# Query and key operands of the scores: transposed and split in the projection stage and stored, instead of in the attention stage

## What is computed

```python
xn = _rmsnorm(x, norm1_w)
proj = xn @ w_in
q, k, v, f_raw, z, xbc, dt_raw, g_att, g_ssm = _split_proj(proj)
q = _rmsnorm(q.reshape(b, T, 16, 64), q_norm_w)
k = _rmsnorm(k.reshape(b, T, 16, 64), k_norm_w)
logf = jax.nn.log_sigmoid(f_raw + b_f)
# attention, per head; c = cumsum(logf), for the running rows over the cached keys too
s = jnp.einsum('bqhd,bkhd->bhqk', q, k) * 64 ** -0.5
s = jnp.where(mask, s + (cq - ck), -jnp.inf)
att = softmax(s) @ v
```

## Time and profile before

| what | value |
|---|---|
| median of three runs | 2890.07 us (2890.05 to 2894.38) |
| the profiled execution's own time | 2885.89 us |
| its span, first to last instruction | 2884.1 us |
| PE busy over the span | 2737.1 us (95%) |
| DVE / ACT / POOL busy | 1577.2 (55%) / 1022.4 (35%) / 405.7 us (14%) |
| mean granted TensorE clock | 0.978 of full speed |
| DMA | 273.31 MB, mean 95 GB/s |

### The profile page before, as it was taken

One profiled execution on the slowest core, in us unless ns is written; L12 is line 12 of the kernel. 1 busy time (PEld: TensorE's weight loads), 2 busy tenths in 40 slices (PEclk: granted clock), 3 DMA queues, 4 the chain that ended last, 5 costly groups with the idle time before them and its releaser, 6 DMA issues. The chain is left out here.

```text
span 2884.1 us, 47789 instructions
## 1 busy us (share of the span) xinstructions
PE 2737.1 (95%) x18754; PEld 2658.0 (92%) x18754; DVE 1577.2 (55%) x2867; ACT 1022.4 (35%) x2353; POOL 405.7 (14%) x475
## 2 busy tenths in 40 slices
PE   6998979999999999997999989998989999999999
PEld 5997978989999889887999979998989999999999
DVE  4336337656566565565898864464373444434434
ACT  4223336556666655653434331121231111111110
POOL 0000012212122222222555520000000000000000
PEclk8999999999999999998999999999989999999999
DMA  3222232132232222215888873343221111111112
GB/s 115 90 90 53 79 90 91 43 101 76 67 108 76 66 93 58 84 63 140 205 194 214 201 203 121 112 134 128 65 99 58 45 44 45 44 45 44 48 67 96
DMA packets 334448, 273.31 MB, mean 95 GB/s; under 512 B 95952, under 2 KB 311632, under 8 KB 334096
## 3 DMA queue, kind: packets, MB, share of 16 engines
q1 hardware_dynamic: 334224, 270.25, 32.9%
HBM read 197.90 MB, written 72.28 MB: 94 GB/s over the span
## 5 line engine op out<-in xcount | busy, mean ns | idle before, releaser
L411 PE MATMUL banks<-w_hi,xn_hi 128*128 128x256 f32 x1440 | 407.8, 287 | 8.7 <-DVEq L368 5.0
L411 PE MATMUL banks<-w_lo,xn_hi 128*128 128x256 f32 x1440 | 405.5, 286 | 0.0
L414 PE MATMUL banks<-xn_hi,w_hi 128*128 128x352 f32 x1152 | 379.5, 329 | 0.7 <-ACT att_xs L986 0.7
L414 PE MATMUL banks<-xn_hi,w_lo 128*128 128x352 f32 x1152 | 378.7, 329 | 0.0
L414 PE MATMUL banks<-xn_lo,w_hi 128*128 128x352 f32 x1152 | 378.2, 328 | 0.0
L411 PE MATMUL banks<-w_hi,xn_lo 128*128 128x256 f32 x1280 | 366.3, 286 | 0.0
L411 PEld LDWEIGHTS banks<-w_hi,xn_hi 128*128 128x128 f32 x1440 | 276.7, 192 | 10.6 <-DVEq L368 5.1
L411 PEld LDWEIGHTS banks<-w_lo,xn_hi 128*128 128x128 f32 x1440 | 276.6, 192 | 0.2
L1704 PE MATMUL banks<-h_hi,w_hi 128*128 128x352 f32 x768 | 248.8, 324 | 1.9 <-DVEq L1625 1.9
L1704 PE MATMUL banks<-h_lo,w_hi 128*128 128x352 f32 x768 | 248.6, 324 | 0.0
L1704 PE MATMUL banks<-mlp_uhi,w_hi 128*128 128x352 f32 x768 | 248.6, 324 | 0.0
(11 more groups left out here) (293 smaller groups left out, 6160.8 us busy)
## 6 DMA issues: line engine op xcount, KB each, us to landing
w_raw<-in_w_in SPq DMA_DIRECT2D x44, 1024.0 KB, 5.5
scratch_xbc<-att_co SPq DMA_DIRECT2D x32, 512.0 KB, 2.6
ssd_ab<-scratch_acum SPq DMA_DIRECT2D x64, 256.0 KB, 6.0
br_g<-scratch_gates SPq DMA_DIRECT2D x72, 176.0 KB, 2.8
scratch_gates<-hand_tanh SPq DMA_DIRECT2D x48, 176.0 KB, 5.4
scratch_z<-att_z_stage SPq DMA_DIRECT2D x64, 128.0 KB, 1.9
ssd_xbc<-scratch_xbc SPq DMA_DIRECT2D x64, 128.0 KB, 3.4
ssd_xbc<-scratch_xbc SPq DMA_DIRECT2D x128, 64.0 KB, 3.7
```

The lines of the kernel that those rows point to most:

```text
L411: ins = self.nc.tensor.matmul(self.bank(n, P, PW), x[:, k, t * P:(t + 1) * P], w[:, k, :], start=first, stop=end)
L414: ins = self.nc.tensor.matmul(self.bank(n, P, TT), w[:, k, m * P:(m + 1) * P], x[:, k, r * TT:(r + 1) * TT], start=first, stop=end)
```

## The change

In `project_qkv` the normed q and k are now also transposed, for two heads at once, split into hi and lo with the factor 1/8 and q's norm weight, and stored as `q_ops` and `k_ops` (per head 64 rows, 64 rows and the four bias rows). The cached keys go the same way in slots 0 to 3. There are 44 such groups: four for the cache and five for each of the eight q and k panels. PE transposes the group of a panel that ended at slot e in slots e + 4 to e + 8, behind the tile of that slot, all into one bank (4); ACT rounds it (`turned_hi`) and DVE makes the low part (`turned_lo`) in the slot after; SP stores it. For the next group PE waits until the low part of the one before is made. `sq` holds one tile now and DVE sums tile by tile; the weight multiplication is left out for q.

In `attention_z_xbc` the loads of q and k, the transposes, `make_hi`, `make_lo` and `double` are gone, and so is all work of POOL. SP loads each operand group with two DMAs (`load_ops`). Its bank becomes a third one for tiles. The low parts of the 24 panels are made by DVE.

```diff
 class HeadNormTm:
+    GROUPS = 5
+    CACHED = 4
+    B_TURNED = 4
...
-        self.sq, self.ss = sb("sq", [P, NT + 1, PW]), sb("ss", [P, (NT + 1) * self.HEADS])
+        self.sq, self.ss = sb("sq", [P, PW]), [sb(f"ss{x}", [P, (NT + 1) * self.HEADS]) for x in range(2)]
...
+    def groups(self, i, n):
+        out = []
+        if i == 0 and 0 <= n < self.CACHED:
+            out.append((n, None))
+        for g in range(self.GROUPS):
+            for k in self.ended(n - 4 - g):
+                out.append((self.CACHED + (i * self.per + k) * self.GROUPS + g, (k, g)))
+        return out
...
     def start_sp(self, sp):
+        sp.dma_start(rows.rearrange("p (t n) -> p t n", t=2), self.cache_k.rearrange("(t p) n -> p t n", p=P)).then_inc(self.cached, 16)
...
     def act(self, act, i, n):
...
             s.nc.scalar.activation(self.stage[x][0:m, t, :], s.bank(n, m, PW), ACT.Copy).then_inc(self.copied, 1)
-            s.nc.scalar.activation(self.sq[0:m, t, :], s.bank(n, m, PW), ACT.Square).then_inc(s.free, 1)
+            if u:
+                act.wait_ge(self.summed, u)
+            s.nc.scalar.activation(self.sq[0:m, :], s.bank(n, m, PW), ACT.Square).then_inc(s.free, 1)
+        for c, src in self.groups(i, n - 1):
+            w = self.width(src)
+            act.wait_ge(self.turned, c + 1)
+            if c >= 2:
+                act.wait_ge(self.ops_stored[c % 2], self.landed(c - 2))
+            s.nc.scalar.activation(self.t_hi[c % 2][:, 0:w], s.core.banks[:, self.B_TURNED, 0:w], ACT.Copy,
+                                   scale=self.scale(src)).then_inc(self.hi_made, 1)
...
     def dve(self, dve, i, n):
...
+        for k, t in s.mine(self, n):
+            q, m = i * self.per + k, rows_of(t)
+            if t == 0 and q >= 2:
+                dve.wait_ge(self.scaled, q - 1)
+            s.wait_free(dve, i, n)
+            v.tensor_reduce(self.ss[k % 2][0:m, t * self.HEADS:(t + 1) * self.HEADS], self.sq[0:m, :].rearrange("p (h d) -> p h d", d=HD),
+                            AX.X, ALU.add).then_inc(self.summed, 1)
+        for c, src in self.groups(i, n - 1):
+            w = self.width(src)
+            dve.wait_ge(self.hi_made, c + 1)
+            bank, hi, lo = s.core.banks[:, self.B_TURNED, 0:w], self.t_hi[c % 2][:, 0:w].bitcast(F32), self.t_lo[c % 2][:, 0:w]
+            v.scalar_tensor_tensor(out=lo, in0=bank, scalar=self.scale(src), in1=hi, op0=ALU.mult, op1=ALU.subtract).then_inc(self.lo_made, 1)
...
+    def pe(self, pe, i, n):
+        s = self.stream
+        for c, src in self.groups(i, n):
+            if src is None:
+                pe.wait_ge(self.cached, 16)
+            elif src[1] == 0:
+                self.wait_normed(pe, i, src[0])
+            if c:
+                pe.wait_ge(self.lo_made, c)
+            for rows, m, col in self.blocks(c, src):
+                ins = s.nc.tensor.transpose(s.core.banks[:, self.B_TURNED, col:col + m], rows, s.core.ident[0:m, 0:m])
+            ins.then_inc(self.turned, 1)
...
                 for n in range(stream.slots):
                     stream.pe(pe, i, n)
+                    norm.pe(pe, i, n)
...
-    B_SCORES, B_TURNED, B_PREP, B_OUT, B_TILES = 0, 2, 4, 5, (6, 7)
+    B_SCORES, B_TURNED, B_OUT, B_TILES = 0, 2, 5, (4, 6, 7)
...
-        stream.low_on_pool = True
...
+                    sp.dma_start(first, k_ops[h:h + 1, 0:HD, cols].to_broadcast([2, HD, cols.stop - cols.start])).then_inc(loaded, 16)
+                    sp.dma_start(second[0:KX, :], k_ops[h, HD:HD + KX, cols]).then_inc(loaded, 16)
...
-                for g in prepared(h, u, 1):
-                    prep(h + 1, g)
```

More of the change, by code:

```diff
@@ new lines, in blocks @@
+    def blocks(self, c, src):
+        if src is None:
+            rows = self.stage[1][:].rearrange("p t n -> p (t n)")
+            return [(rows[:, t * D + (2 * c + b) * P:t * D + (2 * c + b + 1) * P], P, (2 * b + t) * P) for b in range(2) for t in range(2)]
+        k, g = src
+        stage = self.stage[k % 2]
+        if g == 4:
+            return [(stage[0:TS, NT, b * P:(b + 1) * P], TS, b * TS) for b in range(2)]
+        return [(stage[:, 4 * (g % 2) + t, g // 2 * P:(g // 2 + 1) * P], P, t * P) for t in range(4)]
@@ new lines, in places, with width @@
+    def places(self, i, c, src):
+        if src is None:
+            return [(4 * c + 2 * b, 1, slice(TP, TP + PAST), b * PAST) for b in range(2)]
+        k, g = src
+        head = (i * (self.per // 2) + k // 2) * self.HEADS
+        first = 0 if k % 2 == 0 else PAST
+        if g == 4:
+            return [(head + 2 * b, k % 2, slice(TP + first, TP + first + TS), b * TS) for b in range(2)]
+        return [(head + g // 2 * 2, k % 2, slice(g % 2 * 512, (g % 2 + 1) * 512), 0)]
+    def width(self, src):
+        return 2 * TS if src is not None and src[1] == 4 else 512
@@ new lines, in wait_normed @@
+    def wait_normed(self, eng, i, k):
+        if k % 2:
+            eng.wait_ge(self.weighted, (i * self.per + k) // 2 + 1)
+        else:
+            eng.wait_ge(self.scaled, i * self.per + k + 1)
+    def start_sp(self, sp):
+        sp.dma_start(self.w[:], self.weights[1].to_broadcast([P, HD])).then_inc(self.w_loaded, 16)
+        with self.stream.nc.allow_non_contiguous_dma(reason="one value per partition"):
+            for b in range(2):
+                sp.dma_start(self.w_q[b * HD:(b + 1) * HD, :], self.weights[0].rearrange("o (d e) -> d (o e)", e=1)).then_inc(self.w_loaded, 16)
+        rows = self.stage[1][:].rearrange("p t n -> p (t n)")[:, 0:2 * D]
+        sp.dma_start(rows.rearrange("p (t n) -> p t n", t=2), self.cache_k.rearrange("(t p) n -> p t n", p=P)).then_inc(self.cached, 16)
@@ L538, in finish @@
+        for c, src in self.groups(i, n - 1):
+            sp.wait_ge(self.lo_made, c + 1)
+            for head, x, cols, col in self.places(i, c, src):
+                at = (HD, 0) if x == 0 else (0, HD)
+                w = cols.stop - cols.start
+                for part, buf in zip(at, (self.t_hi, self.t_lo)):
+                    sp.dma_start(self.ops[x][head:head + 2, part:part + HD, cols], buf[c % 2][:, col:col + w].bitcast(F32)).then_inc(self.ops_stored[c % 2], 16)
     def finish(self, sp):
-        for x in range(2):
-            sp.wait_ge(self.stored[x], 32 * (self.stream.rounds * (self.per // 2) + 1))
+        count = self.CACHED + self.stream.rounds * self.per * self.GROUPS
```

324 lines of the change are left out of this document (104 added, 220 removed).

## The result

| | before | after |
|---|---|---|
| median of four runs | 2890.06 us (2886.37 to 2894.38) | 3113.69 us (3110.36 to 3116.58) |
| ratio to before, with its 95% interval | | 1.0773 [1.0754, 1.0792] |
| PE's first matmul of the projection to its first of the attention stage | 346.6 us | 588.2 us |
| from there to PE's last transpose of that stage (`att_tails`) | 929.8 us | 908.2 us |
| from there to the end of the span | 1566.4 us | 1572.6 us |

The change is 7.7% slower, 224 us. I had said 2900 us, in a range from 2870 to 2926. The attention stage is shorter, as forecast, though by 22 us and not by 61. The projection was to grow by 71 us and grew by 242.

The account below looks back on a forecast made before the run. The prediction took PE, busy 95% of the span, to bound the kernel. Terms of -60.7 us in attention and +71 us in the projection gave +10 us, 2900 us on the median of 2890.07, range 2870 to 2926.

Parts of the forecast that it names:

- At nothing: Costs put at zero: operand stores in the projection, operand loads in the attention stage, and the third bank.
- 1. transposes leave attention: Attention stage: 320 transposes of k and q go, 80 bursts of 0.44 us on PE, -35.2 us.
- 2. and 3. waits of the attention stage: First head's two low-part waits and their clock go, -5.5 us; other attention waits shrink, -20 us with clock.
- 4. transposes in the projection: Projection: 36 bursts of four transposes and 8 of two are added on PE, +18 us.
- 5. waits for the low part: Projection, q panels and cache groups: PE waits for the previous group's low part, 15 times 2.2 us, +33 us.
- 6. clock behind them: Projection: half of the 15 new waits drop the clock to 1.2 GHz, 8 falls of 1.7 us, +13 us.
- 7. second round, slots 9 to 17: Projection: the old 3.4 us wait goes, four new waits fall into the old 10.7 us one; +3 us net.
- 8. start and end: Projection: cached-key load delays the first panel, 3 us; small stores ahead of the barrier, 1 us; +4 us.
- Point 3: Attention waits beyond the first head: POOL silent, fewer loads ahead, -20 us; sign of error: stage shorter by 35 us or less.
- the change does not do what it says: Rival: operand loads land late and PE waits at each head, 15 x 2 us, 2930 us; chance 0.03.
- The faster rival: Nearly all attention waits close, 45 instead of 20 us, and the clock falls in few cases; 2867 us, chance 0.27.
- The rival of a late DVE in attention: 96 new low-part rows on DVE delay reciprocals and maxima, attention wait gain about 0; 2920 us, chance 0.13.

Follow-up runs that it names:

- two_banks_first: both_by_head with high and low parts made ahead of evictions and sums, and transposed groups in two PSUM banks in turn; 2870.32 us, 0.9931 of before.
- both_by_head: The change with its operand stores and the loads of the key's high part each cut in two, one per head; 2932.78 us, 1.016 of before.

## Why the prediction was wrong

**The step that failed** is "At nothing: the stores of the operands (their landing is asked for two groups later)". I gave them two groups of time and no price. Their price is 5.2 us per 256 KB on two DMA engines, and cutting them by head is worth 154 us of the 214 us by which I missed. The row to bound it from was the earlier trace rows: 1 MB of weights in 5.5 us, which would make 256 KB 1.4 us; nothing in the trace of before had a store with two as its slowest dimension, so a bound from above was missing, and the form of the access pattern had to be read. **The same line had the loads at nothing**; with one broadcast load of two copies each they cost 24 us. (What their second loads cost, on four engines, no run shows.) The rest, 2933 against 2900 us, lies in the terms that I did write down. With the stores and loads by head, and two_banks_first (no short waits, clock 0.96 as before) to part busy time from clock:

| step | forecast | measured |
|---|---|---|
| 1. transposes leave attention | -35.2 | -37.7 (PE busy 882.88 to 845.14) |
| 2. and 3. waits of the attention stage | -25.5 with the clock | -6.2 (idle 46.9 to 40.7); the clock's share is in the row above |
| 4. transposes in the projection | +18 | +19.8 (busy 322.45 to 342.23 in two_banks_first) |
| 5. waits for the low part | +33, 15 of 2.2 us | +49.0, 21 pieces |
| 6. clock behind them | +13 | +21.7 (busy 363.95 against 342.23) |
| 7. second round, slots 9 to 17 | +3 | -10.9 (3.2 in place of 14.1 us), but see below |
| 8. start and end | +4 | 3.8 and 4.8 more |
| the stages behind attention | 0 | +4.3, not explained |

```profile
41.45:476.20 434.75, 363.95 (x2750) 355.97 (x2750) 161.25 (x291) 124.51 (x298) 0.00 (x0) 0.92 0.36 100
476.20:1362.00 885.80, 845.14 (x5891) 808.32 (x5892) 535.03 (x920) 514.53 (x1220) 0.00 (x0) 0.98 0.35 103
```

```profile
41.47:409.81 368.34, 342.23 (x2751) 337.27 (x2751) 160.36 (x291) 125.48 (x298) 0.00 (x0) 0.96 0.42 118
```

These are the stretches of both_by_head (both stages) and of two_banks_first (projection). The projection's lines add up: 19.8 + 49.0 + 21.7 + 3.2 - 14.1 + 8.6 = 88.2 us, which is 434.8 - 346.6. And 88.2 - 44.0 + 4.3 = 48.5 us, the difference of the spans (2932.7 - 2884.1) to 0.1 us.

**Point 5** had the mechanism and the size of one wait right (2.06 to 2.11 us, where I had 2.2), in every q panel and at the cache's groups. The number was off: I let the four of the second round's first q panel fall into PE's old wait of 10.7 us. That wait is gone from L731 of the earlier trace rows and came back as the 8.4 us piece at L628, with the others beside it, so **point 7**'s gain of 11 us and nearly all of point 5's excess of 16 us are one misreading. **Point 6:** of 19 pauses of 2.0 to 2.4 us in both_by_head's projection 12 were followed by the 1.2 GHz level. Two of them, one that was not and one that was (PE paused 2.11 us ahead of 110.03 and of 115.67):

```profile
110.30:113.70 3.40, 3.26 (x28) 3.06 (x26) 0.00 (x0) 0.10 (x1) 0.00 (x0) 1.00 0.83 257
116.50:119.90 3.40, 3.40 (x18) 3.40 (x17) 0.00 (x0) 0.00 (x0) 0.00 (x0) 0.50 0.66 157
```

I had taken a half. The Trainium skill, "TensorE: Matmul & The Clock Gate", section "HAM oscillation", has such falls only behind longer pauses; these rows speak against it once more. **Point 3** failed. Its own sign came, a stage shorter by 35 us or less, but 20 us of that were the loads; with these by head the stage is 44 us shorter, and still of 20 us at most 5 came (2.4 of idle time beyond the first head's 3.8, and 2.5 of busy time beyond point 1). Resting POOL and shorter DVE rows are worth nothing that can be measured, and the weights' transfers, which I wanted to see earlier, come later: the stage moves more bytes, and some of its loads keep to four engines; which of the two it is stays open. **The rivals:** "the change does not do what it says" named late operand loads; loads were in fact a cost, but through the weights queued behind them and not at the heads' first scores. The faster rival needed 36 us from point 3 and had no ground. The rival of a late DVE in attention had none either: with the 96 low parts back on POOL the time is the same.

## What to carry to other kernels

Before a DMA is costed at nothing, read the slowest dimension of both its sides and price it by its bytes over that few engines; if its buffer is a ring, the transfers of one group must land in the time in which the program makes a group, however many groups later they are asked for: here 10.4 us against a slot of 3.2. (64 x 5.2 = 333 us against the whole stage's 347 would have looked as if it fitted.) When a stage turns up longer than forecast, follow the wait through all the engines to its last link, and look at the DMA share there: a steady small share with everybody waiting is a transfer of the wrong form, and here another bank did not mend it (a deeper ring was not tried). A change that looks refuted can be a good one with a bad transfer: here the idea was worth 15 us once its two DMA forms and its one PSUM bank were mended, and 20 us with the new order on ACT and DVE too.

## What the runs showed of the hardware that I had not expected

- A store whose DRAM side is `[2, 64, 512]` goes out at 50 GB/s on 2.1 engines (5.2 us for 256 KB); the same bytes as two stores of `[64, 512]` keep three quarters of 16 engines busy, 0.52 MB in 3 us. Cutting it by columns doubles the number and gains nothing (3156 against 3114 us).
- The operands' loads of 68 rows run on 4.0 engines at 86 GB/s, where the stores of 64 rows kept three quarters of 16 engines busy.
- While such stores are queued, one issue of an operand store on SyncE takes up to 5.75 us, where by head its median is 0.6 us and its longest 2.0; transfers behind it start late for that reason too. The change's timeline of SyncE:

```profile
198.13 0.48 SPq L645 DMA_DIRECT2D scratch_k_ops<-qkv_turned_hi  x1
198.65 4.84 SPq L645 DMA_DIRECT2D scratch_k_ops<-qkv_turned_lo  x1
207.84 0.48 SPq L645 DMA_DIRECT2D scratch_k_ops<-qkv_turned_hi  x1
208.76 5.75 SPq L645 DMA_DIRECT2D scratch_k_ops<-qkv_turned_lo  x1
```

- DVE's convolution step at 2.34 us beside a POOL split looked like a tax worth lifting. It was the exception: the mean of all 96 was 1.40 us.
